# Weight parts, the value blend and unread products moved or added around the waits of TensorE in a two-unit, four-layer block

## What is computed

```python
# first unit, layer 0 (rglru_group)
log_a = -LRU_C * r * softplus(-lam); a = exp(log_a)
# sqrt(1 - a*a) scales the input of the recurrence h = a*h + sqrt(1-a*a)*(i*u)
# first unit, both layers
kv = rms_norm(mem, g_mem) @ w_kv; k, v = split(kv)         # "memk", "memv"
s = softmax(q k^T / sqrt(128)); o = s v                    # "xa" attention, 8 units here
x = x + concat([y_mix, y_mem]) @ w_out; x = x + sqrelu_mlp(rms_norm(x, g))
# second unit, layer l
h = rms_norm_2(x, norm1_g[l]) * (1 + sc1) + sh1            # the front norm
p = h @ w_in[l]                                            # slabs lat, gl1, k2, r2, v2, z, g0, g1
v = v + (v_first - v) * sigmoid(v0 + vl @ v_up)            # the value blend, layer 1 only
mixed = sigmoid(g0) * (y_a @ proj_a) + sigmoid(g1) * (y_b @ proj_b)   # slabs pa and pb
x = x + gt1 * (mixed @ w_out); x = x + gt2 * ((silu(gate) * up) @ w_down)
return rms_norm_2(x, final_g)
```

## Time and profile before

| what | value |
|---|---|
| median of three runs | 2796.89 us |
| the profiled execution | 2802.87 us |
| its span, first to last instruction | 2801.3 us |
| TensorE matmul busy | 2711.2 us, 97% |
| VectorE, ScalarE, GpSimd busy | 57%, 35%, 7% |
| chain of work that ended last | TensorE 89%, VectorE 6%, ScalarE 3% |
| mean granted TensorE clock | 0.987 |
| DMA | 281.15 MB, 100 GB/s on the mean |

### The profile page before, as it was taken

How to read it: one execution, slowest core, us unless ns; L and a number is a source line. 1 busy time by engine, 2 the same in 40 slices (tenths; PEclk the granted TensorE clock), 3 DMA queues, 4 the chain that set the end, 5 groups by cost and what they waited for, 6 DMA issues and landing times.

```text
span 2801.3 us, 45290 instructions
## 1 busy us (share of the span) xinstructions
PE 2711.2 (97%) x19179; PEld 2250.6 (80%) x19179; DVE 1593.4 (57%) x2330; ACT 990.4 (35%) x1363; POOL 194.0 (7%) x272
## 2 busy tenths in 40 slices
PE   8989999999899999999999999999989999999998
PEld 6778888888688888777878888888768878888887
DVE  5567777755667777765554553333585454633334
ACT  5653222244632222353332431223433433432223
POOL 5000000000000000001050000000010130000000
PEclk9999999999999999999999999999999999999999
DMA  4233555522035555320023323232220023223231
GB/s 157 91 113 125 184 169 171 170 76 76 1 115 183 176 162 172 100 91 27 4 80 95 101 90 106 91 106 79 75 65 8 25 89 99 91 91 105 91 101 65
DMA packets 238828, 281.15 MB, mean 100 GB/s; under 512 B 9646, under 2 KB 225202, under 8 KB 238642
## 3 DMA queue, kind: packets, MB, share of 16 engines
q1 hardware_dynamic: 225322, 226.28, 25.2%
q0 software_dynamic: 13184, 52.11, 6.3%
q10 hardware_dynamic: 136, 0.03, 0.0%
HBM read 276.30 MB, written 2.10 MB: 99 GB/s over the span
## 4 chain that ended last, share of the span: by engine, by line
PE 89%; DVE 6%; ACT 3%; issue 2%; DMA 0%; ACTq 0%; DVEq 0%; POOL 0%; POOLq 0%
PE psum L2512 25%; PE psum L2513 24%; PE psum L2514 24%; DVE wlo L1618 1%; PE psum L2586 1%; PE psum L2588 1%; PE psum L2587 1%; PE psum L3051 1%; PE psum L3066 1%; ACT whi L908 1%; PE psum L3034 1%; PE psum L3090 1%; PE psum L3023 0%; PE psum L2981 0%; PE psum L2999 0%
## 5 line engine op out<-in xcount | busy, mean ns | idle before, releaser
L2512 PE MATMUL psum<-hh,whi 128*128 128x512 f32 (+1 forms) x2032 | 789.5, 389 | 9.3 <-DVE wlo L1618 6.2
L2513 PE MATMUL psum<-hl,whi 128*128 128x512 f32 (+1 forms) x2032 | 779.9, 384 | 0.0
L2514 PE MATMUL psum<-hh,wlo 128*128 128x512 f32 (+1 forms) x2032 | 779.9, 384 | 0.0
L1618 DVE TENSOR_TENSOR wlo<-raw,whi 128x2048 fp32r<-128x2048 f32 x219 | 503.1, 2298 | 478.7 <-ACT whi L908 478.3
L908 ACT ACTIVATE whi<-raw 128x2048 fp32r<-128x2048 f32 x219 | 418.3, 1910 | 526.5 <-PE psum L2514 522.2
L2512 PE MATMUL psum<-mh,whi 128*128 128x512 f32 (+1 forms) x1248 | 487.5, 391 | 7.5 <-DVE wlo L1618 4.3
L2513 PE MATMUL psum<-ml,whi 128*128 128x512 f32 (+1 forms) x1248 | 480.9, 385 | 0.0
L2514 PE MATMUL psum<-mh,wlo 128*128 128x512 f32 (+1 forms) x1248 | 480.8, 385 | 0.0
L2512 PEld LDWEIGHTS psum<-hh,whi 128*128 128x128 f32 x2032 | 383.5, 189 | 98.0 <-issue 11.6
L2514 PEld LDWEIGHTS psum<-hh,wlo 128*128 128x128 f32 x2032 | 383.3, 189 | 75.6
L2513 PEld LDWEIGHTS psum<-hl,whi 128*128 128x128 f32 x2032 | 383.9, 189 | 73.5 <-issue 0.5
(11 more groups left out here) (468 smaller groups left out, 2731.4 us busy)
## 6 DMA issues: line engine op xcount, KB each, us to landing
rest<-in_ada_w POOLq DMA_DIRECT2D x64, 768.0 KB, 5.3
raw<-in_w_gu SPq DMA_DIRECT2D x44, 1024.0 KB, 5.1
raw<-in_w_in SPq DMA_DIRECT2D x34, 1024.0 KB, 5.2
raw<-in_w_mlp_in SPq DMA_DIRECT2D x32, 1024.0 KB, 5.4
raw<-in_w_mlp_out SPq DMA_DIRECT2D x32, 1024.0 KB, 5.0
raw<-in_w_out SPq DMA_DIRECT2D x16, 1024.0 KB, 5.0
raw<-in_w_down SPq DMA_DIRECT2D x16, 1024.0 KB, 5.0
raw<-in_w_mem_kv SPq DMA_DIRECT2D x8, 1024.0 KB, 5.0
```

The lines of the kernel that those rows point to most:

```text
L1618: ins = dve.tensor_tensor(wlo[:, g % 2, :, :], raw[:, g % 2, :, :], f32(whi[:, g % 2, :, :]), ALU.subtract)
L2512: pe.matmul(out, whi_, xhi, start=first, stop=False)
L2513: pe.matmul(out, whi_, xlo, start=False, stop=False)
L2514: return pe.matmul(out, wlo_, xhi, start=False, stop=last)
```

## The change

Six groups of moves and five kinds of places with added products:
- first unit: block 0 of slab u 1 stands before `rb`; its block 1 behind
- projection: in the gates of the second unit, ScalarE's high part of slab pa stands before the four high parts of y_a, and VectorE's low part between the second and the third low part of y_a
- value slab: `lo` of slab v 0 stands before the factor's reciprocal
- layer 0's attention: the square of a is done by VectorE (as a product) instead of by ScalarE; `hi` of memk 1,0 stands right behind the exp, `lo` behind the square
- the delta rule: `lo` of slab z 0 stands at level 4 instead of level 0; in layer 1 the blends of value tiles 1 and 2 stand at levels 0 and 1 instead of at level 2
- unread products (`idle_products`: the identity times the identity, 128 by 128, into the bank of the job that comes next, which overwrites them): before the first transposes of each attention (6 and 20), before the front norm's mean square (6 and 24), before its `rb` (5, layer 1), before slab lat (14, layer 1), and before the last mean square (14)

```diff
--- before.py
+++ after.py
@@ Plan.walk @@
             if l == 0:
                 self.slab_jobs("u", 0, 0, 2)
+                self.block("u", 0, 1, 0)
                 self.add("rb", 0)
-                self.slab_jobs("u", 0, 1, 2)
+                self.block("u", 0, 1, 1)
@@ ScalarE, layer 0 of the first unit @@
                     act.activation(RB, RB, ACT.Exp).then_inc(S("lru_a"), 1)
-                    act.wait_ge(S("lru_a"), 1)
-                    act.activation(DB, RB, ACT.Square).then_inc(S("lru_a2"), 1)
+                    hi(slab_of("memk", 1, 0))
                     evac_tokens("memv", 0, mV[0], MT_, [0], high=False)
-                    hi(slab_of("memk", 1, 0))
                     evac_tokens("memv", 0, mV[0], MT_, [1], high=False)
                     hi(slab_of("memk", 1, 1))
@@ ScalarE, both layers of the second unit @@
                     free(act.activation(KK[:, b, :], bank(j), ACT.Sigmoid), j)
+                hi(plan.slab["pa", (l, 0), 0])
                 for t in range(4):
                     act.wait_ge(S("ya_gated"), 4 * l + t + 1)
...
-                        hi(plan.slab[name, (l, p), 0] + 1)
+                        if p:
+                            hi(plan.slab[name, (l, p), 0] + 1)
@@ VectorE, layer 0 of the first unit @@
                         dve.tensor_scalar(RB[:, t, :], RB[:, t, :], nsp[:, t:t + 1], None, ALU.mult).then_inc(S("lru_loga"), 1)
-                    lo(slab_of("memk", 1, 0))
                     evacuated(dve, J["igate", 3])
                     dve.tensor_tensor(IB, IB, UC, ALU.mult).then_inc(S("lru_iu"), 1)
+                    dve.wait_ge(S("lru_a"), 1)
+                    dve.tensor_tensor(DB, RB, RB, ALU.mult).then_inc(S("lru_a2"), 1)
+                    lo(slab_of("memk", 1, 0))
                     dve.wait_ge(S("lru_a2"), 1)
@@ VectorE, layer 1 of the first unit @@
+                    lo(slab_of("v", 0))
                     evacuated(dve, J["ms", 2])
                     dve.reciprocal(tk[:, 1, :], tk[:, 0, :]).then_inc(S("token_factor"), 1)
...
-                    lo(slab_of("v", 0))
                     dve.wait_ge(S("token_factor"), 2)
@@ VectorE, both layers of the second unit @@
                     if m == 0:
                         keys_scaled()
-                        lo(plan.slab["z", l, 0])
+                        if l:
+                            values_mixed(1)
                     level_right(m, 0)
...
                         bonus_in(2)
+                        if l:
+                            values_mixed(2)
...
                         bonus_in(3)
-                        if l:
-                            values_mixed(1)
...
                     level_right(m, 2)
-                    if m == 0 and l:
-                        values_mixed(2)
...
                     level_left(m, 4)
                     if m == 0:
+                        lo(plan.slab["z", l, 0])
                         evacuated(dve, J["v2", l, 1, 1])
                         if l:
                             values_mixed(3)
...
+                    if t == 5:
+                        lo(plan.slab["pa", (l, 0), 0])
                     if t >= 3:
                         dve.wait_ge(S("ya_hi"), 4 * l + t - 2)
...
-                    for name in ("g0", "g1") if p else ("g1",):
+                    for name in ("g0", "g1") if p else ():
                         lo(plan.slab[name, (l, p), 0] + 1)
@@ TensorE @@
+            def idle_products(n, *key):
+
+                p = ahead(*key)
+                for _ in range(n):
+                    pe.matmul(p[:, 0:P], ident[:, :], ident[:, :], start=True, stop=True)
...
                     if 0 <= u < units:
+                        if u == 0:
+                            idle_products(20 if l else 6, name + "_t", l, u)
                         pe.wait_ge(S("att_probs"), base + u + 1)
...
                     linear("u", 0, 0, h, before=normed(0))
+                    linear("u", 0, 1, h, only=0)
                     pe.wait_ge(S("x_factor"), 1)
...
-                    linear("u", 0, 1, h)
+                    linear("u", 0, 1, h, only=1)
...
                     modulation_rows(1)
+                idle_products(24 if l else 6, "ms", 4 + 2 * l)
                 mean_square_tokens(4 + 2 * l)
                 if l == 0:
                     modulation_turned(1, 0, ahead("mod", 1))
+                if l:
+                    idle_products(5, "rb", 4 + 2 * l)
                 factor_rows(4 + 2 * l, l + 1)
...
+                if l:
+                    idle_products(14, "lat", l, 0, 0)
                 linear("lat", l, 0, h, before=normed(4 + 2 * l))
...
                 if i == 1:
+                    idle_products(14, "ms", 8)
                     pe.wait_ge(S("norm_added"), 7 * 8)
```

## The result

The changed kernel takes 2772.68 us (median of four runs, 2770.40 to 2773.54); the kernel before took 2798.86 us beside it (four runs, 2796.48 to 2805.78). The ratio on record is 0.9897 with a 95% interval of 0.9882 to 0.9911 (the two medians alone give 0.9906), 1% faster. The profiled execution takes 2772.68 us, its span is 2771.1 us: 30.2 us less than the profiled execution before. The prediction was 28.4 us less, and 2770 us for the median.

What follows compares the result with a forecast made beforehand. TensorE, busy for 97% of the span, was taken as the bound, with gains only at its waits or low clock. Terms sum to -28.4 us: 2774.5 profiled, 2768.5 median, stated as 2770; the 8-in-10 range is 2760 to 2784.

Steps and rivals of the forecast that it cites:

- First unit: Before `rb`: block 0 of slab u 1 fills TensorE's 2.64 us wait; -2.8 us.
- recurrence: Layer 0: square on VectorE and earlier slab parts start the attention's first exp 4.1 us earlier; -4.1 us.
- value slab: Slab v 0: low part ahead of the reciprocal removes a 2.8 us wait and the low clock behind it; -4.3 us.
- slab pa: Both layers: pa's waits of 1.76 and 2.58 us and some low clock go; -3.2 and -2.5 us.
- Rival C: Gains are given back as ScalarE, VectorE or GpSimd sets the next wait; only -8 us, 2789; chance 0.06.
- Delta rule, second layer: Blends ahead of GpSimd's product, less waiting, full clock over the bonus products; -9.0 us, bounds -5 and -10.
- what is late next: +1.5: Second layer's delta rule: slab's low part waits about 2.2 us for GpSimd's second product, partly under bonus products; costs 1.5 us.
- Delta rule, first layer: Slab z's low part no longer precedes the evacuation TensorE awaits, but meets GpSimd's second product; -0.6 us.
- Layer 1's cross-attention: 20 unread products against a 3.64 us wait, with ScalarE and VectorE setting the pace behind; -0.3 us, bounds +1 and -2.
- Front norms: Unread products: first layer's fit the wait, 0; second layer's lengthen the queue but give full clock behind, -2.4 us.
- Rivals B and D: B: moves pay, clock stays 0.50, 2780 median, chance 0.22. D: half-clock products make it slower, about 2801, chance 0.03.
- End: Before the last mean square: 14 unread products take 3.1 us against a 2.08 us wait plus drain; costs 0.8 us.

Runs made afterwards that it cites:

- the first run: All unread products removed from the changed kernel, all moves kept: 2777.69 us, ratio 0.9904.
- with fewer: Unread products reduced or dropped by place, against the changed kernel with slab z 0's low part behind the bonus evacuations: 2768.63 us, ratio 0.9878.
- the second norm's only: Unread products kept only at the second layer's front norm, against the changed kernel with slab z 0's low part behind the bonus evacuations: 2772.10 us, ratio 0.9893.
- the trimmed ones: Unread products cut to the waits, 12 added in layer 0's attention, against the changed kernel with slab z 0's low part behind the bonus: 2769.24 us.

## Why the prediction was right, and where it wasn't

The sum was 28.4, and the steps of the table add up to 28.4. Ten of the eleven terms are within 0.5 us or lie in their bounds; that it came out so exactly is luck, since the larger errors, +1.3, +1.0 and -1.8, nearly cancel. The 1.8 us that the profiles differ more than forecast lie ahead of the change.

- First unit, recurrence, value slab, slab pa: the steps were right, in size too (the table's five steps make 17.3 us, 16.9 forecast), and undone together they cost about what they had brought (17.3 by the medians). Their sizes one by one hold a share of low clock that is chance: of slab pa's 3.2 us in the first layer 1.6 was a low stretch that another execution has at the first unit instead. Rival C, gains given back later, is out. The six products before the attention's first transposes cost nothing, but not for the reason given: they don't stand in front of the 3.89 us wait but one unit ahead of it.
- Delta rule, second layer, forecast -9.0, measured -7.7. The step on the blends is right (undone, 8.4 us). The step that was mis-sized is "what is late next: +1.5". The low part did wait for GpSimd, 2 us, as said; but the two instructions of the fourth blend stand behind it too, and the evacuations began 6 us behind the first bonus product instead of 2. TensorE waited 2.48 us, and a low stretch of 3.4 us (2074.2 to 2077.6) came behind: 4 us instead of 1.5.
- Delta rule, first layer, forecast -0.6, measured +0.4. The wait at the first right level shrank by 0.8, as said. Not foreseen was that the slab's load now starts at 1267 and stands in front of TensorE's code, below: 2.5 us, of which half would have been lost at a like stop a little later anyway (1.45 us at 1297.3 before).
- The new place of the slab's low part, which the prediction itself called a loss by the rule of the Trainium skill on the shared port (SBUF — State Buffer, Who interferes with whom), is what cost both. Put behind GpSimd's products it gives 4.7 us between the profiles, 3.7 by the medians.
- Layer 1's cross-attention, forecast -0.3, measured -2.1, just outside its bound of -2. Turned transposes of q took 1.91 us at full clock instead of 3.62, but the wait behind them grew to 1.34: net -0.9, as argued, ScalarE and VectorE set the pace. The other 1.2 is 3.4 us less of low clock in the 80 us behind it (10.2 before, 6.8 after), which no row of before could tell.
- Front norms: -0.2 and -2.3 against 0 and -2.4. At the first the six products were priced at nothing; the three profiles without them lose 0.9 to 2.1 us there by a longer low clock (1.5 in the first run, 0.9 with fewer, 2.1 with the second norm's only). The price of a product, 0.22, was right, and so was that full clock over dense work pays more than the products' excess. Rivals B and D, clock stays at 0.50, are out: it was 1.00 under the products in every execution, but for 3.4 us with the trimmed ones.
- End: +0.8 as forecast; yet the three profiles without these products differ from those with them by +0.3, +0.5 and -0.7 there, since the clock can fall in the wait instead. It is about even.
- The step from the profile to the median: the profiled execution of before lay 6 us above the median of its three runs, and 4 us above that of the comparison. Going 4.5 us below the sum's own 2774.5 for that was about half right: 2772.7 lies between the two.
- A reading: "each low stretch that the rows show lies behind a wait of 2.8 us or more" does not hold for the trace, nor for the prediction's own rows. The low clock at 1442.2 came behind a wait of 1.76 us, and in the runs above it fell in or behind waits from 0.57 us (1953.9, with the products cut to the waits) to 4.08 us, and stayed up behind one of 2.74 us (142.87, with the slab's low part behind the bonus).

## What to carry to other kernels

Where one engine is busy for 97% of the span, read its waits one by one and ask at each which instruction on the supplying engine stands ahead of the needed one without being needed; these moves add up and stay (17.3 us undone together, where their terms said 16.9). Place VectorE work like these blends and low parts, with two inputs and the output in SBUF, before or behind GpSimd's long instructions, never a microsecond into them: a 0.7 us blend cost 4.9. Filling waits with unread work paid clearly at one place here, where a long wait stands ahead of dense matmuls (2.4 us). Trimming it saved 2.1 us at that place and nothing in the median: a low stretch that goes from one place may turn up at another, and each added instruction of TensorE shifts the places where it stops for code.

## What the runs showed of the hardware that was not expected

TensorE's code is itself a stream that can be late. The queue shown first has 149 packets of 16 KB. That they carry TensorE's code is inferred: they make some 260 of its 2 x 19357 instructions for each. In the delta rule, where 96 matmuls take 1.6 us, such packets follow each other closely (1271.05, 1274.77). The stop at 1271.01 to 1273.51 sits in the middle of 96 like products that wait for nothing. The DMA rows of the changed kernel from 1267.00 to 1271.04 and from 1271.04 to 1273.60 (queue, packets, MB, share):

```profile
q1 hardware_dynamic: 983, 1.00, 74.4%
q0 software_dynamic: 189, 0.35, 24.1%
...
q0 software_dynamic: 99, 0.24, 31.2%
q1 hardware_dynamic: 57, 0.05, 5.7%
q8 instruction: 1, 0.02, 2.5%
```

(The first two rows are those of the first stretch.) The code packet comes when the slab's load (q1) is nearly through, and TensorE goes on 2.46 us after the packet has started. In the changed kernel without its products:

```profile
1278.22 0.56 PE L3063 MATMUL psum<-mo 64*64 64x64 f32 x18
1280.83 0.40 PE L3063 MATMUL psum<-mo 64*64 64x64 f32 x12 [2.05 <-issue]
```

It has 32 products, 128 TensorE instructions, fewer ahead of this place, and the stop comes 61 matmuls (each with its weight load) later: it sits at one place of the code, not of the computation. Its packet starts at 1278.48, 0.01 us after the last packet of the loads, and TensorE goes on 2.35 us later. In the kernel before the same can be seen at 2077.90: the slab's load ends at 2076.70, the code packet starts at 2076.71, and TensorE stops for 1.24 us. With the low part at level 0 or behind the bonus, the same code meets no load there (the load runs from 1249.8 to 1253.7, or from 1270.6 to 1275.1), and the stop of 2.49 is missing. With the low part behind the bonus the packet that answers to the one at 1271.05 starts at 1266.97, while TensorE is at the same instruction within 0.4 us. So a move on VectorE shifted the load that its end releases, and behind the load TensorE's code came 4 us later. That the packet queues behind the load's packets is the reading that fits all of these; the moment at which it is asked for is in no trace, and a run that shifts only the load was not made.

A load ahead is not needed for a stop. With the low part behind the bonus TensorE is idle for 1.27 us before 1348.41, 2.67 us after a code packet, and no DMA ran in the 2.7 us ahead of that packet. Every profile of this study has stops of 0.7 to 1.9 us in both delta rules, idle time with no releaser, and each ends 2.2 to 2.9 us after a code packet has started. (A wait of 0.9 us at L3109, where the packets start at any distance, is not of this kind.) Those behind a load were 1.0 to 2.6. So a change in the number of TensorE's instructions moves these stops and changes their sum, by about 2 us for a delta rule in the two runs above, and this is part of what separates the kernels with more and with fewer products. The Trainium skill (Runtime: NRT & Kernel Launch, Instruction fetch mechanics) says that instructions come in blocks of 16 KiB, 256 of them, and that crossing from one to the next is mostly hidden; the size agrees with the rows, the hiding doesn't hold for matmuls this small.

The low clock stretches wander. Executions of kernels that differ only late in the program had theirs at other places early in it: 142.3 to 145.7 in the changed kernel, 165.9 to 169.3 in the one with the low part behind the bonus, where nothing ahead of 1262 differs. A term for one low stretch (1.5 us) should therefore count as a mean over executions, not as a fixed part of a place.
